# Halved signals for the low weights, a reordered first stage, and rotations moved into the query projections

## What is computed

```python
# first block
mod = silu(c) @ w_ada + b_ada                       # six vectors of 1024
h = rms_norm(x, g) * (1 + scale_m) + shift_m
p = h @ w_in                                        # u_f 512, v, b_g, c_g, g_logits 2 x 1024
y_a = fourier_mix(u_f) @ w_fourier
y_b = (b_g * centred_conv3(c_g * v, w_conv)) @ w_conv_out
z = gate_a * y_a + gate_b * y_b                     # gates: sigmoid of g_logits
x = x + gate_m * (z @ w_o)
# third block, both attentions
q = apply_rope(h @ w_q, cos, sin)                   # 16 heads of 64
k = apply_rope(h @ w_k, cos, sin)
o = softmax(q k^T / 8 + mask) v                     # nsa: plus the branch with 15 compressed keys
```

## Time and profile before

| | us |
|---|---|
| median of 3 runs | 2895.9 (2888.8 to 2897.1) |
| profiled execution | 2894.96, its span 2893.2 |
| TensorE busy (matmuls) | 2526.2 (87%) |
| VectorE busy | 1243.1 (43%) |
| ScalarE busy | 748.5 (26%) |
| chain that ended last | PE 54%, DMA 21%, SyncE's queue 11% |
| data moved | 720.69 MB, mean 249 GB/s |

### The profile page before, as it was taken

One profiled execution on the slowest core, in us unless ns is written; L12 is line 12 of the kernel. 1 busy time (PEld: TensorE's weight loads), 2 busy tenths in 40 slices (PEclk: granted clock), 3 DMA queues, 4 the chain that ended last, 5 costly groups with the idle time before them and its releaser, 6 DMA issues.

```text
span 2893.2 us, 34910 instructions
## 1 busy us (share of the span) xinstructions
PE 2526.2 (87%) x14300; PEld 1749.7 (60%) x14300; DVE 1243.1 (43%) x1829; ACT 748.5 (26%) x1087; POOL 21.1 (1%) x37
## 2 busy tenths in 40 slices
PE   7989867677777777799989999999989999996998
PEld 4888313122222221278677998788957888884887
DVE  2354200000000000033533776876566778765676
ACT  3332000000000000013222334434254334344433
POOL 1000000000000000000000000000000000000000
PEclk8999876777677767799899999999989999998999
DMA  8666999999999999954333554554403546541453
GB/s 311 225 226 236 418 417 416 417 418 419 418 416 418 418 418 418 416 212 160 124 117 122 196 176 168 177 193 168 152 16 118 202 160 204 183 166 58 162 187 116
DMA packets 272068, 720.69 MB, mean 249 GB/s; under 512 B 11200, under 2 KB 128976, under 8 KB 238816
## 3 DMA queue, kind: packets, MB, share of 16 engines
q1 hardware_dynamic: 270000, 708.88, 64.8%
q0 software_dynamic: 1968, 10.38, 1.0%
HBM read 716.08 MB, written 3.15 MB: 249 GB/s over the span
## 4 chain that ended last, share of the span: by engine, by line
PE 54%; DMA 21%; SPq 11%; issue 8%; DVE 4%; ACT 2%; DVEq 0%; POOLq 0%; POOL 0%; ACTq 0%
SPq L721 10%; PE bank L1311 9%; PE bank L929 7%; DMA ring<-in_w_gate_e 5%; DMA A<-in_w_gate_e 4%; PE bank L1312 4%; PE bank L860 4%; PE bank L862 4%; PE bank L861 4%; DMA xn<-in_w_up_e 4%; PE bank_pair L860 4%; PE bank_pair L861 4%; PE bank_pair L862 4%; DMA ring<-in_w_up_e 2%; DMA ring<-in_w_in 1%
## 5 line engine op out<-in xcount | busy, mean ns | idle before, releaser
L1312 PE MATMUL bank<-HT_r,ring_r 128*128 128x256 f32 x1408 | 395.7, 281 | 0.0
L1312 PEld LDWEIGHTS bank<-HT_r,ring_r 128*128 128x128 f32 x1408 | 266.8, 189 | 0.7
L2317 DVE TENSOR_TENSOR A<-bank,A 128x512 f32<-128x512 f32 x16 | 11.1, 692 | 585.5 <-PE bank L1125 585.5
L862 PE MATMUL bank<-HT_r,ring_r 128*128 128x256 f32 x904 | 255.7, 283 | 0.0
L1311 PE MATMUL bank<-HT_r,AB_r 128*128 128x512 f32 x640 | 229.4, 402 | 1.4 <-DVE HT_r L2069 1.4
L1311 PE MATMUL bank<-HT_r,AC_r 128*128 128x512 f32 x640 | 226.5, 398 | 0.0
L2060 DVE TENSOR_TENSOR ring_r<-ring,AB_r 128x2048 fp32r<-128x2048 f32 (+1 forms) x80 | 177.5, 2260 | 103.1 <-ACT AB_r L1635 102.0
L1125 PE MATMUL bank<-ring,A 128*32 128x512 f32 x768 | 143.7, 838 | 85.3 <-DMA ring<-in_w_gate_e 48.5
L2060 DVE TENSOR_TENSOR ring_r<-ring,A_r 128x2048 fp32r<-128x2048 f32 (+1 forms) x82 | 175.8, 2182 | 15.3 <-ACT A_r L1635 15.3
L862 PE MATMUL bank_pair<-A_r 128*128 128x512 f32 x456 | 179.1, 393 | 0.0
L861 PE MATMUL bank_pair<-ring_r,A_r 128*128 128x512 f32 x448 | 174.5, 390 | 0.0
(11 more groups left out here) (479 smaller groups left out, 4505.9 us busy)
## 6 DMA issues: line engine op xcount, KB each, us to landing
ring<-in_ffn_w_gu SPq DMA_DIRECT2D x88, 1024.0 KB, 6.7
ring<-in_w_up_e SPq DMA_DIRECT2D x48, 1024.0 KB, 26.6
ring<-in_w_gate_e SPq DMA_DIRECT2D x48, 1024.0 KB, 22.2
ring<-in_w_down_e SPq DMA_DIRECT2D x48, 1024.0 KB, 19.5
ring<-in_w_in SPq DMA_DIRECT2D x46, 1024.0 KB, 7.4
ring<-in_ffn_w_down SPq DMA_DIRECT2D x40, 1024.0 KB, 6.4
A<-in_w_gate_e SPq DMA_DIRECT2D x32, 1024.0 KB, 18.9
A<-in_w_up_e SPq DMA_DIRECT2D x32, 1024.0 KB, 26.6
```

The source lines that it names most:

```text
L862: return mm(out_, lhs[1], rhs[0], start=False, stop=stop, skip_group_check=True)
L1312: last = mm(both[:, 1, :], low, h_high[:, k, :], start=False, stop=(k == DC - 1), skip_group_check=True)
```

## The change

Five things are edited; what is computed stays the same.

1. VectorE signals `low_ready` after each half; TensorE waits for the first at the slab's start and for the second at the first matmul that reads it.
2. x, the identity (the first 128 columns of `consts`) and the rest of `consts` get a DMA and a semaphore each; the rest is issued after `uf`'s slab is in. The input's transposes stand behind the second modulation slab and go to banks 0 to 3. ScalarE squares x ahead of the second modulation's copy.
3. The convolution is made in two parts behind the low halves of `in7` and `in8`; cast and subtraction stay behind that of `in9`.
4. The low half of the second `conv_out` slab stands behind z's first group, that of `w_o0` behind the second; `w_o0` waits for z group by group.
5. In both attentions three query rotations stand between the third and the fourth query batch, the fourth behind half of the compression (NSA) or behind the scores of head pair 0 (window). NSA's scores of pair 0 stand ahead of the compressed scores, and its first weighings between the steps of the compressed softmax. In the window attention scores wait for the rotation of their own heads.

```diff
@@ make_plan
+        if m == 1:
+            p.add("norm0", "AAAA")
-    p.add("norm0", "WWWW")
...
+            p.add("nsa_q", "W" * 7, [1, 6], split=2)
+            p.add("cmp_hid0", "W")
+            p.add("nsa_rope3", "W")
+            p.add("cmp_hid", "W", [0])
             p.add("cmp_kv", "WW")
+            p.add("nsa_scores0", "AA")
             p.add("cmp_s", "WW")
...
+            p.add("swa_q", "W" * 7, [1, 6], split=2)
+            p.add("swa_scores0", "A")
+            p.add("swa_rope3", "W")
@@ tensor
         def split_slab(name, s, it=0):
-            pe.wait_ge(S["low_ready"], split_number(name, s, it))
+            number = split_number(name, s, it)
+            pe.wait_ge(S["low_ready"], 2 * number - 1)
...
             def at(c, n):
+                if c >= second and not whole:
+                    whole.append(pe.wait_ge(S["low_ready"], 2 * number))
...
         for m in range(4):
             modulation(m)
             modulation_sum(m)
-        pe.wait_ge(first_loaded, N_FIRST)
-        normT(1, "norm0")
+            if m == 1:
+                first_normT()
...
+        def z_ready(k):
+            if k % 2 == 0:
+                pe.wait_ge(S["z_ready"], k // 2 + 1)
+        to_acc3("w_o0", 0, z_high, z_low, 0, ready=z_ready)
...
+        def turn_q(name):
+            for i in range(3):
+                copied(pe, name, Q_AT[i])
+                rope(name, Q_ROPE_AT[i], pairs(q3, i))
+
+        feature_major3("nsa_q", 0, 0, h_parts)
+        feature_major3("nsa_q", 2, 1, h_parts, between=lambda: turn_q("nsa_q"))
...
         def swa_scores(m):
+            pe.wait_ge(S["rope_ready"], 9 + m // 2)
...
         swa_scores(0)
+        copied(pe, "swa_q", Q_AT[3])
+        rope("swa_rope3", 0, pairs(q3, 3))
@@ gpsimd
+        pool.dma_start(x[:, :, :], dram("x").rearrange("(t p) d -> p t d", p=P)).then_inc(x_loaded, 16)
+        pool.dma_start(consts[:, 0:P], dram("consts")[:, 0:P]).then_inc(ident_loaded, 16)
...
         loaded(pool, "uf", 0)
+        pool.dma_start(consts[:, P:n_const], dram("consts")[:, P:n_const]).then_inc(tables_loaded, 16)
@@ vector
         for s in range(8):
             low(f"in{s + 1}", 0)
...
+            if s == 6:
...
+                link(v.tensor_tensor(f_bc[:, :, :], f_cv[:, :, :], ...
+                for c in range(DC):
+                    ins = v.scalar_tensor_tensor(f_bc[:, c, 1:T], f_cv[:, c, 0:T - 1], col("w_conv", c),
+                                                 f_bc[:, c, 1:T], ALU.mult, ALU.add)
+            if s == 7:
...
+                link(v.tensor_tensor(f_bc[:, :, :], f_bc[:, :, :], f_b[:, :, :], ALU.mult))
...
+            if i == 0:
+                low("conv_out", 1)
+            if i == 1:
+                low("w_o0", 0)
```

198 lines of the change are left out of this document (96 added, 102 removed).

## The result

| | before | after |
|---|---|---|
| median, us | 2895.3 (2888.8 to 2897.1) | 2860.1 (2856.6 to 2862.9) |
| ratio | | 0.9882, interval 0.9867 to 0.9898 |
| profiled execution | 2894.96 | 2862.86 |
| TensorE busy | 2526.2 | 2506.4 |

The change takes 35.2 us off the median and 32.1 off the profiled execution, which was the slowest of the four. Forecast were 26.4 us and 2869. The direction and most of the mechanisms held. What the sum left out or put too low is the question of the rest.

What follows compares the result with a forecast made beforehand. Bounds: DMA in the expert stretch, TensorE in the first stage's projections. First stage 16.9 less 0.9 at the start, NSA 3.2 and window attention 7.2 make 26.4 us off 2894.96: 2868.6, stated as 2869; range 2860 to 2883.

Steps and rivals of the forecast that it cites:

- The halves: First-stage slabs: low halves signalled by halves shrink each wait by about 1.5 us, 5.1 us gained over four small waits.
- The price of nothing for the 116 waits: Mid-slab waits, one in each of 116 slabs: 0.01 us or nothing each; rival of 13 us in all, chance 0.05.
- Convolution, Fourier product and its clock: Fourier product: 6.73 us wait goes but for 0.35, clock gives 2.2, new wait before the next modulation part costs 2.4.
- z: Before the output product: the 3.07 us wait for z's low half goes, and 2.5 us of low clock behind it.
- The start: Kernel start up to uf: tables out of the first loads, transposes moved forward; 0.9 us lost, ends 0.5 gained, 5.3 lost.
- the walk: Start, stepped forward: fourth modulation slab copied at about 35.2, uf ending 21.3 us later, at 56.8 against 55.9.
- Through the experts: DMA-bound expert stretch: its loads begin when the last output product is done, so all 16.0 us go through.
- The rival in which the gain stops there: Expert stretch: its loads keep their times, only the attentions count, 10.4 us gained, 2885; chance 0.07.
- NSA: NSA attention: rotations moved into the projection and compression, pair 0 scores ahead of compressed scores; 3.2 us gained, ends 0 and 3.8.
- the three waits: NSA attention: 0.75 us for an exponential, 2.15 for the first weighed probabilities, 0.89 for the last query copy; 3.8 us.
- Window attention: Window attention: first scores need rotation 0 only; 7.2 us gained, 5.2 if VectorE's fourth rotation doesn't hide.
- three terms (0.89, 5.38, 0.92): Window attention: query copy 0.89 us, VectorE alone finishing the rotations 5.38, fourth rotation off the path 0.92.

Runs made afterwards that it cites:

- the kernel with 1368 more: The changed kernel with 1368 more waits on TensorE, all already met, 555 of them comparing with a register: 2858.5 us, ratio 0.9887.
- the first stage alone: The changed kernel with both attentions as before, keeping the first stage, its start and the halves: 2878.7 us, ratio 0.9946 against the kernel before.

## Why the prediction held, and where it was off

**The halves: 5.1 forecast, 6.9 measured** at w_o0 with the halves undone, of which 4.2 are waits, 2.1 go with low clock behind them and 0.6 are a later DFT that may be chance. Alone, on the old kernel, they give 5.7 us from the DFT to the Fourier product. The 5.3 at the end of w_o are near the forecast by luck, as w_o's clock was high in that profile. The price of nothing for the 116 waits holds, as the kernel with 1368 more shows.

**Convolution, Fourier product and its clock: 6.2 net forecast, 5.8 measured** at w_o0 (7.4 at its end). The new wait came at its place with 2.81 instead of 2.4 us. The step that had no term is the clock behind it: the modulation product took 0.7 us more than the others and the next slab ran at 0.92, so that the wait cost 4.4 us and not 2.4.

**z: 5.6 forecast, 6.3 measured** at the end of w_o. The output product started at 239.45, forecast 239.5.

**The start: 0.9 lost forecast, 1.0 gained measured** in the first pair of profiles. The step that failed is that the walk hangs everything on the fourth modulation's copy. In after the copy came at 33.1 and not at 35.2, as the clock rose within the transposes (5.23 us, not 6.6). In the second profile of the same kernel the transposes took 6.75 us and the copy came at 34.6, and the DFT began at the same time all the same. What the two share is the rounding of uf's weights, which begins at 34.8 and 35.1; in after ScalarE waits 1.10 us for their DMA. Before, it began at 36.89, also behind a wait for that DMA. So taking the tables out of the first loads, which the walk used only for the third modulation slab, brought the weights some 2 us sooner (with the start undone the rounding begins at 36.69). Half of that reached the DFT: TensorE, idle ahead of uf, began it at the low clock (0.62 from 42 to 47 us; before, uf ran at 1.00), as the walk had it. The walk also adds up wrongly by 0.3: 35.2 + 21.3 is 56.5. How much of the 1.0 us is the start's own is open, between nothing and all of it, as the run with the start undone says.

**Through the experts: all of it, as forecast.** The rival in which the gain stops there, 2885, is out: the first stage alone gave 16.3 us at the end. The 1.4 us by which the first two profiles differ there are not the change's.

**NSA: 3.2 forecast; 4.8 in the first profile, 6.6 on the mean of ten. The mis-sized term.** Counted were the three waits, 3.8 us less a loss of 0.6. Between the end of the projection and the first transposes 28.9 us became 18.2; less the three rotations that now lie inside the projection (2.75, at 0.92 each) that is 8.0 us gained. Of these the waits make 3.8. Nearly all of the rest is the clock of the work behind them: the compressed scores took 6.29 us and take 4.21, the two scores of pair 0 took 4.3 and take 2.4. In the windows of PE the stretch from the last compression product to the last scores of pair 0, of before:

```profile
2093.90:2106.10 12.20, 10.98 (x61) 0.58 0.56 174
```

and in after the same work with one more group of scores, the first of pair 1:

```profile
2073.20:2083.10 9.90, 9.36 (x74) 0.85 0.66 214
```

At the Fourier and the output product I had put a price on the low clock behind a wait; here, where the same row could be had, I had not. Part of the gain is given back in the head loop, which before took 68.8 to 68.9 us and now takes 67.4 to 72.2 from profile to profile, at more or less of the high clock.

**Window attention: 7.2 forecast; 7.4 in the first profile, 9.6 on the mean.** What its three terms (0.89, 5.38, 0.92) stand for is gone. Between the end of the projection and the first transposes 17.2 us became 6.0; less 2.75 for the rotations that moved, that is 8.4, so 1.2 more than the terms. The text had named "1 to 2 us more if the clock stays up" and left them out of the sum. In the first profile the head loop itself ran at a low clock (windows of PE, after, then the same kernel's second profile):

```profile
2597.80:2640.00 42.20, 29.93 (x184) 0.72 0.04 12
```

```profile
2600.00:2639.00 39.00, 24.47 (x184) 0.88 0.04 13
```

3 us between two executions of one kernel, without any difference in its order. So the 7.4 of the first profile, near the forecast, hold 8.4 gained ahead of the loop and 2.0 lost in it (40.4 us before, 42.4 here). That stretches like this one make up the spread of whole executions is likely but was not followed run by run.

**The sum.** Of the 8.8 us that were missing in the forecast, the attentions hold 5.8 on the mean (16.2 against 10.4), the start 1.9, and the first stage behind it 0.8 (17.7 against 16.9). That account takes the attentions from the mean of ten profiles and the rest from the first pair, so it holds to 1 or 2 us. Within the first stage the close match hides two misses: from the DFT to the Fourier product 11.7 us gained against 11.5 forecast, from there to w_o0 1.9 against 2.9, inside w_o 4.2 against 2.5, and the last differs by 1.6 from profile to profile. In the range, low clocks stood only on the slow side. An estimate: the 4 us that the low clock cost in NSA before, taken off the lower end as well, would have let the range begin near 2856.

## What to carry to other kernels

A wait of TensorE that is removed gives back more than itself wherever the work behind it ran at the low clock: for each such wait look in the profile at the granted clock of the work behind it, and put both into the sum, at every place and not only at the largest. A new wait has to be charged in the same way: the one of 2.8 us cost 4.4. Signalling a producer's result by halves is worth the time in which the consumer works on the first half, at each slab where the chain is late; a wait that was already met cost less than 0.01 us here. After such a reordering look for what now stands first in the other engine's queue: here a low half stood ahead of three short products that it did not need, and moving it gave 3.0 to 4.4 us more by the profiles. And one profile of a kernel is not enough to say what a microsecond belongs to: unchanged stretches of this one differ by 1 to 5 us between executions.

## What the runs showed of the hardware

- A semaphore wait on a matmul that is already met costs less than 0.01 us: 203 more of them in a block of 187.49 us left it at 187.49 (187.08 to 187.49 in all profiles), constants and registers alike.
- The granted clock of a stretch with short gaps is not the same from one execution to the next. The head loop of the window attention ran at 0.72 or 0.88 in two profiles of the same kernel (42.4 and 39.3 us), that of NSA took 67.4 to 72.2 us in ten profiles, and w_o, in which TensorE then has no wait over 0.3 us, 27.4 to 30.6 us in ten, with its last part at a clock of 1.00, 0.79 or about 0.67. What decides between them no run here shows.
- The time in which the DMA engines stream the experts is steady to 0.2% in thirteen profiles (961.5 to 963.1 us; the fourteenth has 960.3), and what the stage ahead of it gains goes through it: 18.7 us ahead of it and 17.3 behind in the first pair.
